# Factors spread over partitions by transposes in place of products with the identity

## What is computed

```python
def rms_norm(x, g):
    xf = x.astype(jnp.float32)
    y = xf * lax.rsqrt(jnp.mean(xf * xf, axis=-1, keepdims=True) + NORM_EPS)
    return (y * g.astype(jnp.float32)).astype(x.dtype)

def head_group_norm(o, g):              # per head, over its 64 channels
    ...
    y = (of - mu) * lax.rsqrt(var + GN_EPS)

q = rope(rms_norm_2(q, q_norm), pos)    # second stack: a norm per head
k_w = rope(rms_norm_2(k_all[:, :, 2], k_norm[2]), pos)

p = jax.nn.softmax(s, axis=-1)          # attention: divide by the row's sum
o_s = jnp.einsum('bcghnl,bcgnld->bcghd', p, vg)
```

## Time and profile before

| | |
|---|---|
| time, median of 3 runs | 3457.82 us (3455.53 to 3458.55) |
| the profiled execution: its time | 3452.8 us |
| its span, first to last instruction | 3451.0 us |
| TensorE busy | 3334.1 us, 97% of the span |
| VectorE, ScalarE, GpSimd busy | 1539.2, 1209.5, 748.5 us |
| mean granted clock of TensorE | 0.989 of full |
| DMA | 330 MB, 96 GB/s |

### The profile page before, as it was taken

The page is one execution under the profiler, slowest core; times in us unless marked ns, Lnnn a source line. Parts: engine busy times, 40 slices in busy tenths (PEclk is TensorE's granted clock), DMA queues, the critical chain, the costliest instruction groups (busy, mean ns, idle before and its releaser), DMA issues.

```text
span 3451.0 us, 40740 instructions
## 1 busy us (share of the span) xinstructions
PE 3334.1 (97%) x15941; PEld 2595.3 (75%) x15941; DVE 1539.2 (45%) x1958; ACT 1209.5 (35%) x1652; POOL 748.5 (22%) x390
## 2 busy tenths in 40 slices
PE   7999999999999999999999999989999998999999
PEld 5888776678887888786578887746788877468887
DVE  4444445445545543334543335445433345453333
ACT  4332311543323333335543323245322232652221
POOL 6677500057676740000000000020000002100000
PEclk9999999999999999999999999999999999999999
DMA  6544421144444542221123323201223341013322
GB/s 198 157 147 150 143 74 50 37 135 146 146 145 148 156 124 91 92 86 39 35 80 94 95 97 92 73 25 37 78 93 97 97 91 62 1 50 97 98 97 73
DMA packets 324130, 330.00 MB, mean 96 GB/s; under 512 B 29617, under 2 KB 284721, under 8 KB 323633
## 3 DMA queue, kind: packets, MB, share of 16 engines
q1 hardware_dynamic: 309424, 278.02, 26.4%
q0 software_dynamic: 14592, 50.44, 4.6%
HBM read 326.27 MB, written 2.15 MB: 95 GB/s over the span
## 4 chain that ended last, share of the span: by engine, by line
PE 46%; DVE 2%; ACT 1%; issue 1%; DVEq 0%; ACTq 0%
PE ps L357 18%; PE ps L585 15%; PE ps L565 2%; PE ps L424 2%; PE ps L838 1%; PE ps L865 1%; PE ps L875 1%; PE ps L505 1%; PE ps L476 1%; PE ps L1514 1%; PE ps L845 0%; PE ps L381 0%; ACT w_hi L306 0%; PE ps L373 0%; PE ps L462 0%
## 5 line engine op out<-in xcount | busy, mean ns | idle before, releaser
L310 DVE TENSOR_TENSOR w_lo<-raw,w_hi 128x2048 fp32r<-128x2048 f32 x246 | 604.9, 2459 | 567.4 <-ACT w_hi L306 567.0
L357 PE MATMUL ps<-h_hi,w_hi 128*128 128x512 f32 x2064 | 806.7, 391 | 2.5 <-DVE xT L2047 2.5
L357 PE MATMUL ps<-h_hi,w_lo 128*128 128x512 f32 x2064 | 803.8, 389 | 0.0
L357 PE MATMUL ps<-h_lo,w_hi 128*128 128x512 f32 x2064 | 803.7, 389 | 0.0
L306 ACT CAST w_hi<-raw 128x2048 fp32r<-128x2048 f32 x247 | 471.3, 1908 | 926.0 <-PE ps L357 665.7
L585 PE MATMUL ps<-a_hi,w_hi 128*128 128x512 f32 x1344 | 524.0, 390 | 10.7 <-DVE act L2020 6.2
L585 PE MATMUL ps<-a_hi,w_lo 128*128 128x512 f32 x1344 | 523.0, 389 | 0.0
L585 PE MATMUL ps<-a_lo,w_hi 128*128 128x512 f32 x1344 | 523.0, 389 | 0.0
L357 PEld LDWEIGHTS ps<-h_hi,w_hi 128*128 128x128 f32 x2064 | 388.0, 188 | 84.5 <-issue 4.4
L357 PEld LDWEIGHTS ps<-h_lo,w_hi 128*128 128x128 f32 x2064 | 388.0, 188 | 81.1 <-issue 1.0
L357 PEld LDWEIGHTS ps<-h_hi,w_lo 128*128 128x128 f32 x2064 | 387.9, 188 | 81.0
(11 more groups left out here) (296 smaller groups left out, 3978.9 us busy)
## 6 DMA issues: line engine op xcount, KB each, us to landing
raw<-in_ffn_w_in SPq DMA_DIRECT2D x176, 512.0 KB, 5.0
raw<-in_w_ff SPq DMA_DIRECT2D x128, 512.0 KB, 4.3
m_in<-in_w_mod POOLq DMA_DIRECT2D x96, 512.0 KB, 4.2
raw<-in_ffn_w_out SPq DMA_DIRECT2D x88, 512.0 KB, 4.1
raw<-in_hyb_w_in SPq DMA_DIRECT2D x28, 512.0 KB, 4.6
raw<-in_w_in SPq DMA_DIRECT2D x28, 512.0 KB, 4.7
raw<-in_sb_w_in SPq DMA_DIRECT2D x24, 512.0 KB, 4.4
raw<-in_w_out SPq DMA_DIRECT2D x16, 512.0 KB, 4.5
```

What stands on the lines that cost most here:

```text
L310: eng.tensor_tensor(w_lo[:, e % 2], raw[:, e % 2], w_hi[:, e % 2].bitcast(F32), ALU.subtract).then_inc(s["w_lo_done"], 1)
L357: mm = pe.matmul(ps[:, bank], wbuf[a][:, e % 2, at:at + P], hbuf[b][:, k], start=(k == 0 and n == 0), stop=(k == KC - 1 and n == 2))
```

## The change

The three calls of `pe.matmul` with the identity become calls of `pe.transpose` with the same operands, the same place in PSUM and the same semaphores. No instruction is moved on any engine, and none added or taken away in the program as it is written (TensorE's program has the same 7083 rows in the same order).

```diff
--- before.py
+++ after.py
@@ -407,8 +407,7 @@
             c.chain += chain
             pe.wait_ge(s["norm_chain"], c.chain)
             for b in range(TB):
-                mm = pe.matmul(ps[:, bank, b * P:(b + 1) * P], of[:, b:b + 1].to_broadcast([P, P]), C("ident"),
-                               start=True, stop=True)
+                mm = pe.transpose(ps[:, bank, b * P:(b + 1) * P], of[:, b:b + 1].to_broadcast([P, P]), C("ident"))
             mm.then_inc(s["bcast_done"], 1)
 
         def pe_first_proj(pe, c):
@@ -781,8 +780,8 @@
 
             for b, m in hn_width(x):
                 at = 8 * j + 2 * b
-                mm = pe.matmul(o[:, b * P:b * P + m], r[0:m, at:at + 2].rearrange("p h d -> p (h d)"),
-                               C("ident")[0:m, 0:m], start=True, stop=True)
+                mm = pe.transpose(o[:, b * P:b * P + m], r[0:m, at:at + 2].rearrange("p h d -> p (h d)"),
+                                  C("ident")[0:m, 0:m])
             mm.then_inc(s["hn_bcast"], 1)
 
         def dve_hn_scale(eng, c, x, o, gain):
@@ -842,9 +841,8 @@
                     pe.wait_ge(s["att_rec"], ag + 1)
                     pe.wait_ge(s["att_w"], ag)
                     for I in range(TB):
-                        mm = pe.matmul(ps[:, r_bank(ag), I * P:(I + 1) * P],
-                                       rec_wide(c)[:, I].rearrange("p o d -> p (o d)"),
-                                       C("ident"), start=True, stop=True)
+                        mm = pe.transpose(ps[:, r_bank(ag), I * P:(I + 1) * P],
+                                          rec_wide(c)[:, I].rearrange("p o d -> p (o d)"), C("ident"))
                     mm.then_inc(s["att_r"], 1)
                 if i == 0:
                     wait_projections(pe, c)
```

## The result

| | before | changed |
|---|---|---|
| median | 3457.39 us (3448.80 to 3463.44, 7 runs) | 3442.96 us (3437.67 to 3449.67, 7 runs) |
| ratio, 95% interval | | 0.9960 (0.9945 to 0.9975) |
| profiled execution: span | 3451.0 us | 3443.7 us |
| its mean granted clock | 0.989 | 0.985 |

The changed kernel is 14.4 us faster by the medians, 0.4%; forecast were 16.3. The two profiled executions differ by 7.3 us only.

The account below looks back on a forecast made before the run. TensorE's stream, busy 97% of the span, was taken as the bound. Attention 9.6, layer norms 4.1 and head norms 4.7 made 18.4 us, less 2.1 for the clock: 16.3 off 3457.8 gives 3441.5 us, range 3434 to 3449.

Parts of the forecast that it names:

- What a block costs: Attention block of four on TensorE: 0.91 us as products, 0.42 as transposes, so 0.49 us back; norm blocks taken to halve.
- the fourfold transpose: Rival: every block shrinks to a quarter, 0.23 us in the attention; 26.4 us gained, 3431 us; chance 0.03.
- the transpose that waits for the one before: Rival: each transpose waits for the previous one's end, 1.16 us a block; 10.7 us slower, 3468 us; chance 0.01.
- doesn't do what it says: Rival: the transposes still take two passes; 0 us gained, 3458 us; chance 0.02.
- Attention, 9.6 us: Inverse sums in 20 attention blocks, the first counted half: 19.5 x 0.49 us comes off TensorE's stream.
- The rival in which the waits take this share: In the attention, waits for ScalarE and VectorE absorb the gain: 9.6 us lost, 3451 us; chance 0.08.
- Layer norms, 4.1 us: Eleven layer-norm blocks, one hidden: 10 x 0.41 us, six in the projection's stream and four waited for by VectorE.
- Head norms, 4.7 us: Sixteen head-norm blocks, six hidden: the ten in TensorE's stream give back 0.47 us each.
- The clock, 2.1 us: Allowance for one more half-clock stretch on TensorE, at places with less multiplying between waits: 2.1 us lost.
- The sign given for it: Mean granted clock near 0.989 in the changed kernel; 0.003 lower would mean one or two more half-clock stretches.
- the rival in which the clock keeps part of the gain: Transposes cause 4 to 8 more half-clock stretches, losing 8 to 17 us; chance 0.06 of landing within 0.2% of no change.

Follow-up runs that it names:

- The split's move: Changed kernel with the first half of VectorE's weight split (L328) in the four waiting norms moved behind the norm's own work; also called split behind the wait; ratio 0.9955.
- The single parts: Kernel before with one of the change's three hunks each: attention ratio 0.9985, head norms 0.9992, layer norms 1.0004.
- the layer norms alone: Kernel before with only the layer norms' factor (L410) as transposes; ratio 1.0004.
- the flood with transposes: Changed kernel with the four transposes of the third norm issued 100 times over; 3491.23 us in one run.
- those with doubled transposes: Kernel before with one part's products each as transposes issued twice: layer norms ratio 0.9999, head norms 1.0001, attention 0.9993.
- the flood with products: Kernel before with the four products of the third norm issued 50 times over; 3499.45 us.
- the attention alone: Kernel before with only the attention's inverse sums (L845) as transposes; ratio 0.9985.

## Why the prediction was right, point by point

The time forecast, 3441.5 us, is 1.5 us from the median, and the range held it. Part of this closeness is luck: measured once more, the medians lie 9.8 us apart and not 14.4, 6.5 us from the forecast gain, and the clock took more than was allowed for. The slow end of the range is 3449.7 by its own sum (3457.8 - 8.1), not 3449.

**What a block costs: right.** 0.41 us was measured where 0.42 was taken from the old transposes (0.35 in five of the norms). Half was the factor, and not a quarter: the fourfold transpose is out, so is the transpose that waits for the one before, and so is "doesn't do what it says".

**Attention, 9.6 us: right.** The groups are 0.50 us shorter with TensorE busy throughout. 20 x 0.50 = 10.0 us, the first group included, whose share the trace doesn't separate from the clock. The rival in which the waits take this share is out.

**Layer norms, 4.1 us: the four waited for were wrong.** "The factor is waited for and comes earlier by the whole amount" is the step that failed. The chain named L410 because it ended 0.03 us before VectorE's next instruction, but the half split on VectorE ended in the same moment, and I didn't look at what stood on the waiting engine. Six norms, one at 0.40 and five at 0.46 us, give 2.7 us, and the four gave 0.08 us each. The split's move brought 0.37 us of each back, which settles the cause.

**Head norms, 4.7 us: right.** The pair at 601 us gives 0.92 us (its distance to the next matmul, 1.79 us before and 0.87 after); those at 2221 and 2884 us, each with one of the two small products, give 1.07. At 2238 us the block pair is hidden, as said: the next matmul stands 4.74 us behind its start before (2238.40 to 2243.14) and 4.74 us after (2238.00 to 2242.74).

Sum by what was measured: 10.0 + 2.7 + 0.3 + 3 x 0.92 + 2 x 1.07 = 17.9 us against 18.4. The 0.92 for the pairs at 2192 and 2852 us is taken over from 601, since half clock lies on them in one profile or both.

**The clock, 2.1 us: mis-sized.** I allowed for one stretch, though I named three places that might lose the clock, at 2192, 2221 and 2901 us, and all three did (2190.4, 2224.5 and 2896.9 us above). The sign given for it was wrong too: a mean clock 0.003 lower isn't one or two stretches but 10 us of 3450. In the three groups of runs, the kernel before gives 87 pairs of time and clock; a straight line through them has 3.0 us for each 0.001 of mean clock. The changed kernel's clock in its second measurement is 0.0029 lower, about 8.7 us. With the 9.8 us between the medians there (3454.72 and 3444.96) that makes 18.5 us at equal clock, close to the 17.9 by the rows. The single parts come out by the same sum: 5.2, 2.8 and -1.4 us by their ratios, and 4.5, 2.7 and 4.2 by their clocks, make 9.7 us for the attention, 5.5 for the head norms and 2.8 for the layer norms, where the rows have 10.0, 4.9 and 3.0. These are estimates, each with an interval of several us from its ratio. In the first measurement 17.9 - 14.4 = 3.5 us are left for the clock. The seven runs' mean clock there, 0.9857, lies 0.0024 to 0.0028 below that of before in the three groups, which would be 7 to 8 us; the clocks of before in that measurement are not on record, so this difference stays open. So 2.1 us were forecast for this term, and it cost about 9 where both clocks are known.

Of the rival in which the clock keeps part of the gain the mechanism was right and the reason given for it, transposes, wrong: they hold the clock as well as products. What is shown for one kind of place is the longer wait. In the profiles of the changed kernel (two), of the layer norms alone and of the flood with transposes, TensorE's loads wait 2.2 us behind the norms, and 9 of the 16 have a half-clock stretch behind them. In the ten other profiles the wait is 1.9 us or less, and none of 40 has one; two of those ten are the changed kernel with only this wait shortened. The longer wait alone doesn't decide it: in the four profiles the third norm never has a stretch behind it, the first and the last always do.

**Left open.** The largest new stretch, 13.7 us at 2159.5, stands in a stage (L504 and L1512) that no edit touches. The second profile of the changed kernel, the flood with transposes and the two single parts for norms have it too. But three kernels no shorter than before, those with doubled transposes, have 10.2, 6.8 and 3.4 us there, the flood with products 3.4, the attention alone and the split behind the wait 6.8; the other three, two of them of the kernel before, have none. Whether the shorter programs fall into it more often, or these few profiles only happen to show it, isn't settled; nor is where the attention alone loses its 0.0015 of clock, since it has one profile. And the norms' stretches are a small part of the loss: the profile of the split behind the wait has none of them, and still a mean clock of 0.985.

## What to carry to other kernels

An fp32 product that only copies, with the identity as one operand, costs two passes, and a transpose of the same operands one; where the stream of TensorE is the bound the difference comes off the time. Before a wait is credited with a gain, read what the waiting engine itself does up to its end: a second cause that ends in the same moment swallows it. And where TensorE sits between waits, a shorter piece of work can cost clock; the mean granted clock of all runs belongs beside every comparison below one per cent, and a few filling matmuls or a shorter chain behind the piece keep the wait from growing (what this was worth in the total stayed inside the intervals here).

## What the hardware showed unexpectedly

- 396 extra transposes in a row hold the full clock: 1.00 over 43 us, 0.109 us from start to start.
- TensorE's wait behind a norm grew from 1.8 to 2.2 us (by its weight loads), and half-clock stretches of 3.4 us appeared behind 9 of 16 such norms, after none of 40; each costs about 1.6 us, more than the 0.46 us that a norm's block gives.
- The mean clock of unchanged code varies from 0.986 to 0.991 between runs, at 3.0 us for each 0.001: of the 19 us between its fastest and slowest run (3444.59 and 3463.80 in one group) some 15 are clock.
